# Odd block of a two-block transformer kernel: order of gate and group products, and TensorE at the borders of four stages

## The chip, the cores and the metric

The kernel runs on one core of one Trainium2 chip. The metric is the device time of one execution in microseconds; three executions of the kernel before gave 3166.43 to 3172.95, with a median of 3169.97.

## What is computed

The reference runs two small networks on one sequence of 1024 tokens with 1024 channels, all in fp32: an even and an odd mixer (`first_block`), then a gated linear attention and a forgetting attention with their gated projections (`second_block`). The change is in the odd mixer alone:

```python
def odd_mixer(h, p, on_grid):
    z = h @ p["w_in"]                                  # 1024 -> 4096
    u, g = jnp.split(z, [W_POOL], axis=-1)             # 2048 and 2048 channels
    rows = n // GRID_W
    d = multiscale_pool(u.reshape(bn * rows, GRID_W, W_POOL)).reshape(bn, n, W_POOL)
    d = d.reshape(bn, n, N_POOL_GROUPS, POOL_GROUP_DIM)    # 4 groups of 512
    y = jnp.einsum("bngi,gij->bngj", d, p["w_grp"]).reshape(bn, n, W_POOL) * p["scale"]
    return (y * jax.nn.silu(g)) @ p["w_out"]           # 2048 -> 1024
```

`multiscale_pool` takes, in group g, a mean over a window of 2, 4, 8 or 16 tokens of a row of 64, less the token itself.

## The kernel before

**Layout.** Channels lie on the 128 partitions and tokens along the free dimension, so a tensor of 1024 channels is 8 tiles of 128x1024. A product is made of fp32r parts: each operand is a high part and a low part (`h_hi`, `h_lo`), and `project` (lines 647 to 663) issues three matmuls of 128x512 for each of 8 input tiles and each half of the tokens, 48 for one output tile. A group product has only 4 input tiles (`kts=4`), so 24. Matmuls write to four PSUM slots of two banks each, `slot(0)` to `slot(3)`.

**Weight stream.** All weights pass through one stream of tiles whose order is written out in `STREAMS` (lines 35 to 50). SP loads raw tile n into `wst[n % 2]` (`load_tile`, line 485) when tile n-2 has been split (`w_split`, line 487; the DMA is line 491). GpSimd splits it into `wh` and `wl` (`split_tile`, line 566: one cast, line 585, and four quarter subtractions, line 590) when it has landed and TensorE has used tile n-2, whose buffers it takes (`w_used`, line 583). TensorE waits for the split in `take` (line 665). The order in which TensorE takes tiles is therefore also the order on SP's and on GpSimd's queue. A tile is 1024 columns wide, one for a group product is 512.

**Odd block, stages.** It runs in two parts of two groups each: `odd_a` (groups 0 and 1), `oout_a` (the output projection of their 8 y tiles), `odd_b` (groups 2 and 3), `oout_b`. In each group (`odd_groups`, line 959) TensorE makes

- u0, u1, u2, u3: four projections into slots 0 to 3. ScalarE copies each from PSUM into `up` by halves (line 1621), and VectorE pools each half in a chain of adds, one longer from group to group (lines 2322 to 2334), and splits it into `d_hi` and `d_lo` (lines 2339, 2340). A half of `up` is filled only when VectorE is done with the one before (`o_up`). VectorE signals the end of a tile's pooling with `o_d` (line 2341).
- then four times a gate projection G_j (48 matmuls, slot 2j % 4) and a group product Y_j (24 matmuls on `d`, slot (2j+1) % 4): G0 Y0 G1 Y1 G2 Y2 G3 Y3. Y0 first waits for all four pooled tiles (`o_d`, line 983). ScalarE takes the silu of G_j into `gs` (line 1629), VectorE multiplies Y_j, the scale and the silu (line 2347), signals `o_y`, splits the product into `y_hi` and `y_lo` (lines 2350, 2351) and signals `o_gs` (line 2352).

**Output projections.** `out_phase` (line 994) for `oout_a` makes 8 output tiles of 48 matmuls into slots 0 and 1 in turn. VectorE adds each to the residual stream `xr` (`residual`, line 2193, signal `x_added`), which ScalarE has loaded from DRAM at the stage's start by 8 transfers (line 1637) and stores again (line 1650). The PE waits for `x_added` of the tile two before (line 952). `oout_b` goes by halves of the tokens (`out_by_halves`, line 694): 16 steps of 24 matmuls over four banks; ScalarE loads `xr` in two transfers (line 1375), VectorE adds in line 2249, and TensorE waits for the addition of the step four before (line 701).

**Borders.** Stages are listed in `PHASES` (line 254). Each of TensorE, ScalarE and VectorE signals its end of a stage (`end`, line 263) and `begin` (line 257, its wait is line 261) lets an engine into stage k when all three have ended k-1. Before, TensorE passes such a border ahead of `oout_a`, `odd_b` and `oout_b` (lines 1003, 1005, 1007). ScalarE ends `oout_a` only when the last store of x has landed (line 1653). `xr` and `d_hi`, `d_lo` are the same memory.

Of the kernel before, what the change touches and what calls it, by code (L numbers as in the profile page):

```python
# [22 lines left out]
KT = D // P  # L23
# [8 lines left out]
KB = 1024  # L32


STREAMS = [
    ("w_even_in", 4, [1024, 1024, 1024, 512, 1024, 1024] * 2),
    ("w_even_out", 4, [1024] * 4),
    ("w_odd_in_a", 2, [1024] * 4 + [1024, 512] * 4),
    ("w_odd_out_a", 4, [1024] * 2),
    ("w_odd_in_b", 2, [1024] * 4 + [1024, 512] * 4),  # L40
    ("w_odd_out_b", 4, [1024] * 2),
    ("w_gla_rank", 1, [1024]),
    ("w_gla_in", 4, [1024] * 6),
# [64 lines left out]
def build(nc, dram, out):  # L108
# [24 lines left out]
    nm = sb("nm", 16, vend + 1024)  # L133
# [110 lines left out]
    first, n = {}, 0  # L244
# [183 lines left out]
    def _(sp):  # L428
# [80 lines left out]

        for name, times, widths in STREAMS:  # L510
            if name == "w_fox_in":
                fox_pair(0, widths)
                fox_pair(1, widths)
                with sp.Fori(0, times - 2) as i:
                    fox_pair(i + 2, widths)
                for c in range(2):
                    store_max(times - 1, c)
                    load_max(times - 1, c)
                continue
            if name == "w_even_in":  # L520

                pieces = {3: (0, 1), 4: (2, 3), 5: (4, 5), 6: (6, 7)}
                for j, w in enumerate(widths):
                    load_tile(name, 0, j, EVEN_AT[j], w, widths)
                    if j == 1:
                        for c in range(NEARLY, NCHUNK):
                            load_chunk(c)
                    if j == 3:

                        sp.wait_ge(S("h_ready"), KT)  # L530
                    for n in pieces.get(j, ()):
                        load_piece(n)
                with sp.Fori(0, times - 1) as i:
                    for j, w in enumerate(widths):
                        load_tile(name, i + 1, j, EVEN_AT[j], w, widths)
                continue
            if name == "w_even_out":
                for n, (kind, c, m) in enumerate(EVEN_OUT):
                    sp.wait_ge(S("w_split"), first[name] + n + 1)
                    b = wbuf(name, n)  # L540
                    at = (2 * kind + m % 2) * T
                    sp.dma_start(wst[b][:, :], dram[name][m // 2 * P:(m // 2 + 1) * P, at:at + T])\
                        .then_inc(S(f"w_loaded{b}"), 16)
                continue
            for half in range(passes(name)):
                with sp.Fori(0, times) as i:
                    for j, w in enumerate(widths):
                        load_tile(name, i, j, sum(widths[:j]) if name != "w_even_in" else EVEN_AT[j], w, widths,
                                  half * times * len(widths))
        sp.wait_ge(S("out_stored"), 16 * 5)  # L550

# [81 lines left out]
    def _(pe):  # L633
# [322 lines left out]
                    j += 1  # L956


        def odd_groups(part):
            nm = "w_odd_in_" + "ab"[part]  # L960

            def group(i, chase=False):
                g = 2 * part + i
                act = lambda n: pe.wait_ge(S("o_act"), 8 * g + n)
                yev = lambda n: pe.wait_ge(S("o_y"), 4 * g + n)
                if chase:
                    act(7)
                    yev(3)
                    two_tiles("eout", nm, [(0, 0), (1, 2)], lambda c: half_added("eout", 12 + c),
                              [lambda: take(nm, i, 0), lambda: take(nm, i, 1)])  # L970
                for j in range(2 if chase else 0, 4):
                    (act, yev)[j % 2](7 + j // 2 if j % 2 == 0 else 3 + j // 2)
                    take(nm, i, j)
                    project(j % 2, slot(j), h_hi, h_lo).then_inc(S("w_used"), 1)
                for j in range(4):
                    a, b = 2 * j % 4, (2 * j + 1) % 4
                    act((9, 11, 13, 14)[j])
                    take(nm, i, 4 + 2 * j)
                    project(0, slot(a), h_hi, h_lo).then_inc(S("w_used"), 1)
                    act(10) if j == 0 else act(12) if j == 1 else yev(3 + j)  # L980
                    take(nm, i, 5 + 2 * j)
                    if j == 0:
                        pe.wait_ge(S("o_d"), 4 * g + 4)
                    project(1, slot(b), d_hi, d_lo, kts=4).then_inc(S("w_used"), 1)
            if part == 0:
                group(0, chase=True)
                group(1)
            else:
                with pe.Fori(0, 2) as i:
                    group(i)  # L990
            pe.wait_ge(S("w_used"), first["w_odd_out_" + "ab"[part]] + 2)
            end(pe)

        def out_phase(nm, ready, stat, after, operand=(y_hi, y_lo)):
            with pe.Fori(0, 4) as i:
                out_pair(nm, i, [(*operand, ready)], "x_added", 2)
            pe.wait_ge(S("w_used"), first[after] + 2)
            if stat is not None:
                stats(stat)
            end(pe)  # L1000

        odd_groups(0)
        begin(pe, "oout_a")
        out_phase("w_odd_out_a", None, None, "w_odd_in_b")
        begin(pe, "odd_b")
        odd_groups(1)
        begin(pe, "oout_b")
        out_by_halves("oout_b", "w_odd_out_b", lambda c: None, (y_hi, y_lo))


        def gla_free(c):
# [307 lines left out]
    def _(act):  # L1319
# [290 lines left out]
        def odd_groups(part):  # L1610
            nm = "w_odd_in_" + "ab"[part]

            def group(i):
                g = 2 * part + i
                w0 = first[nm] + 2
                ev = lambda ins: ins.then_inc(S("o_act"), 1)
                for j in range(4):
                    act.wait_ge(S("w_used"), w0 + j + 1 + i * 12)
                    for b in range(2):
                        act.wait_ge(S("o_up"), 8 * g + 2 * j + b + 1)  # L1620
                        ins = A(up[:, :].rearrange("p (r c) -> p r c", c=80)[:, :, 8:72],  # L1621
                                bank(2 * j + b).rearrange("p (r c) -> p r c", c=64), ACT.Copy)
                        ins.then_inc(S("o_u"), 1)
                    act.wait_ge(S("o_u"), 8 * g + 2 * j + 2)
                    act.sem_inc(S("o_act"), 1)
                for j in range(4):
                    act.wait_ge(S("w_used"), w0 + 5 + 2 * j + i * 12)
                    act.wait_ge(S("o_gs"), 4 * g + j + 1)
                    ev(A(gs[j % 2][:, :], slot(2 * j % 4), ACT.Silu))
            with act.Fori(0, 2) as i:  # L1630
# [311 lines left out]
    def _(dve):  # L1942
# [366 lines left out]
        def odd_groups(part):  # L2309
            nm = "w_odd_in_" + "ab"[part]  # L2310
            v3 = lambda t: t[:, :].rearrange("p (r c) -> p r c", c=80)
            for i in range(2):
# [27 lines left out]
                        line(TT_(r3(dl), o3, r3(dh).bitcast(F32), ALU.subtract))  # L2340
                    dve.sem_inc(S("o_d"), 1)
                for j in range(4):
                    dve.wait_ge(S("w_used"), w0 + 6 + 2 * j)
                    dve.wait_ge(S("o_act"), 8 * g + 13 + j)
                    t = gs[j % 2][:, :]
                    m = 4 * i + j
# [426 lines left out]
```

## Time and profile before

| | before |
|---|---|
| median of 3 runs | 3169.97 us (3166.43 to 3172.95) |
| profiled execution, its own time | 3172.45 us |
| its span in the trace | 3170.3 us |
| mean granted TensorE clock | 0.973 of full |
| busy: TensorE, VectorE, GpSimd, ScalarE | 2962.7, 1746.6, 1316.3, 1088.0 us |
| odd block in the trace | about 847 to 1526 us |

How to read it: the profiled execution is one run, traced; its span lacks 2.2 us that its own time has around it. A row of a timeline has the start, the length, engine and line, the tiles out<-in, and in square brackets how long the engine had been idle and what ended that. Matmul records overlap: a row is 0.39 us long while the next begins 0.23 us later, and their ends are modelled.

### The profile page before, as it was taken

The numbers are of one execution on the slowest core, as the hardware profiler recorded it, in microseconds if no ns is written. First come the engines' busy times: TensorE is split into PE (matmuls) and PEld (weight loads), VectorE is DVE, ScalarE is ACT, GpSimd is POOL, SyncE is SP. The second block draws the span as 40 slices with busy tenths as digits, with TensorE's granted clock in tenths as the row PEclk, the third lists the DMA queues.
The fourth block names the chain that finished last, engine by engine and source line by source line (L and its number), as shares of the span: only waits on it lengthen the run. The fifth ranks groups of instructions, "written<-read, shape, count | busy, mean of one in ns | idle before, by whom it ended". The sixth has DMA issues, their size and how long they took to land.

```text
span 3170.3 us, 40111 instructions
## 1 busy us (share of the span) xinstructions
PE 2962.7 (93%) x13930; PEld 2287.7 (72%) x13930; DVE 1746.6 (55%) x2284; ACT 1088.0 (34%) x1429; POOL 1316.3 (42%) x1638
## 2 busy tenths in 40 slices
PE   5999999989999999989899999998999999997997
PEld 3688888757788777867688877776667666665775
DVE  7688999955545116534632322535555655556353
ACT  5344444342211000001332221324455555665232
POOL 2344454447644434436422324775221121211575
PEclk9999999999999999999899999999999999999999
DMA  7412222344311321113301103333222212221423
GB/s 298 161 63 64 63 76 73 114 151 162 102 49 44 116 80 37 47 39 137 107 27 34 33 27 106 96 87 131 54 47 54 48 33 48 48 34 41 140 82 111
DMA packets 113294, 258.56 MB, mean 82 GB/s; under 512 B 24624, under 2 KB 38000, under 8 KB 112384
## 3 DMA queue, kind: packets, MB, share of 16 engines
q1 hardware_dynamic: 83456, 189.43, 20.5%
q10 hardware_dynamic: 29696, 67.21, 5.9%
q8 instruction: 92, 1.51, 0.2%
q14 instruction: 50, 0.41, 0.0%
HBM read 223.97 MB, written 32.64 MB: 81 GB/s over the span
## 4 chain that ended last, share of the span: by engine, by line
PE 75%; DVE 11%; ACT 6%; POOL 4%; issue 3%; DMA 2%; DVEq 0%; POOLq 0%; SPq 0%; ACTq 0%
PE ps L660 20%; PE ps L661 19%; PE ps L662 19%; POOL t_wl L590 3%; PE ps L1212 2%; PE ps L1229 1%; DVE ps L2117 1%; PE ps L1027 1%; PE ps L1028 1%; PE ps L1029 1%; POOL t_wh L585 1%; DVE t_ptl L2580 1%; PE ps L1249 1%; ACT t_pr L1848 1%; DVE t_pb L2327 1%
## 5 line engine op out<-in xcount | busy, mean ns | idle before, releaser
L660 PE MATMUL ps<-t_h_hi,t_wh 128*128 128x512 f32 x2464 | 1011.6, 411 | 43.9 <-POOLq L593 13.5
L585 POOL CAST t_wh<-t_wst 128x1024 fp32r<-128x1024 f32 (+2 forms) x306 | 313.6, 1025 | 1712.1 <-PE ps L662 1538.9
L661 PE MATMUL ps<-t_h_lo,t_wh 128*128 128x512 f32 x2464 | 982.7, 399 | 0.0
L662 PE MATMUL ps<-t_h_hi,t_wl 128*128 128x512 f32 x2464 | 981.9, 398 | 0.0
L590 POOL TENSOR_TENSOR t_wl<-t_wst,t_wh 128x256 fp32r<-128x256 f32 (+2 forms) x1224 | 926.1, 787 | 24.5
L660 PEld LDWEIGHTS ps<-t_h_hi,t_wh 128*128 128x128 f32 x2464 | 467.8, 190 | 196.7 <-issue 60.5
L661 PEld LDWEIGHTS ps<-t_h_lo,t_wh 128*128 128x128 f32 x2464 | 469.0, 190 | 112.7 <-issue 8.5
L662 PEld LDWEIGHTS ps<-t_h_hi,t_wl 128*128 128x128 f32 x2464 | 467.6, 190 | 112.2
L2117 DVE SCALAR_TENSOR_TENSOR ps<-t_upad,t_vec,ps 128x1024 f32<-128x1024 f32 x224 | 275.5, 1284 | 7.1 <-DVE ps L2111 0.9
L660 PE MATMUL ps<-t_y_hi,t_wh 128*128 128x512 f32 x512 | 208.4, 407 | 21.7 <-DVEq L264 14.6
L661 PE MATMUL ps<-t_y_lo,t_wh 128*128 128x512 f32 x512 | 205.6, 402 | 0.0
L662 PE MATMUL ps<-t_y_hi,t_wl 128*128 128x512 f32 x512 | 205.2, 401 | 0.0
L1353 ACT ACTIVATE t_tmp<-t_xr 128x512 f32<-128x512 f32 x96 | 60.7, 633 | 338.6 <-DVE t_xr L2249 154.9
L1848 ACT ACTIVATE t_pr<-t_pr 128x512 f32<-128x512 f32 (+1 forms) x192 | 96.8, 522 | 225.9 <-DVE t_pr L2569 224.7
L2569 DVE SCALAR_TENSOR_TENSOR t_pr<-ps,t_negct,t_abc 128x512 f32<-128x512 f32 (+1 forms) x192 | 109.4, 611 | 68.0 <-PE ps L1233 56.2
L2580 DVE TENSOR_TENSOR t_ptl<-t_pr,t_pth 128x512 fp32r<-128x512 f32 (+1 forms) x192 | 123.1, 682 | 38.0 <-ACT t_pth L1852 37.7
L660 PEld LDWEIGHTS ps<-t_y_hi,t_wh 128*128 128x128 f32 x512 | 98.4, 192 | 50.1 <-DVEq L264 10.8
L2347 DVE SCALAR_TENSOR_TENSOR t_gs<-ps,t_vec,t_gs 128x1024 f32<-128x1024 f32 x16 | 20.5, 1284 | 188.8 <-PE ps L662 188.8
L661 PEld LDWEIGHTS ps<-t_y_lo,t_wh 128*128 128x128 f32 x512 | 98.6, 192 | 24.2 <-issue 0.7
L2554 DVE CUSTOM_DVE_ANT_0 ps<-ps,t_negc 128x512 f32<-128x512 f32 (+3 forms) x128 | 73.3, 612 | 77.5 <-PE ps L1212 44.3
L1621 ACT ACTIVATE t_up<-ps 128x512 f32<-128x512 f32 x32 | 19.2, 599 | 281.3 <-PE ps L662 150.5
L662 PEld LDWEIGHTS ps<-t_y_hi,t_wl 128*128 128x128 f32 x512 | 98.2, 192 | 24.1
(350 smaller groups left out, 4267.4 us busy)
## 6 DMA issues: line engine op xcount, KB each, us to landing
t_wst<-w_even_in SPq DMA_DIRECT2D x40, 512.0 KB, 3.5
t_wst<-w_ple SPq DMA_DIRECT2D x64, 320.0 KB, 2.9
t_wst<-w_even_out SPq DMA_DIRECT2D x32, 512.0 KB, 3.6
t_wst<-w_fox_in SPq DMA_DIRECT2D x32, 512.0 KB, 3.6
t_modw<-w_mod SPq DMA_DIRECT2D x6, 2048.0 KB, 16.2
t_xr<-x_d ACTq DMA_DIRECT2D x6, 2048.0 KB, 11.6
t_wst<-w_gla_in SPq DMA_DIRECT2D x24, 512.0 KB, 3.8
t_wst<-w_odd_in_a SPq DMA_DIRECT2D x16, 512.0 KB, 3.6
```

What stands on the lines that cost most here:

```text
L585: pool.tensor_copy(wh[b][:, 0:w], wst[b][:, 0:w]).then_inc(S("w_high"), 1)
L590: pool.tensor_tensor(wl[b][:, c], wst[b][:, c], wh[b][:, c].bitcast(F32), ALU.subtract).then_inc(S("w_low"), 1)
L660: pe.matmul(o, w1, x1, start=start and k == 0, stop=False)
L661: pe.matmul(o, w1, x2, start=False, stop=False)
L662: last = pe.matmul(o, w2, x1, start=False, stop=stop and k == kts - 1)
L1212: last = pe.matmul(bank(r + hh, 0, (hi - lo) * P), B[x][rows, a], B[y][rows, b], start=(x + y == "qhkh"), stop=(x == "ql" and hi <= t))
L1353: A(sq_half(t), xh(*divmod(t, 8)), ACT.Square).then_inc(S("half_sq"), 1)
L1848: A(pr[x][:, 0:n], pr[x][:, 0:n], ACT.Exp).then_inc(S("f_exp"), 1)
L2117: line.go(STT(out=o, in0=s, scalar=w, in1=acc[a] if o is acc[a] else by_half(acc[a]), op0=ALU.mult, op1=ALU.add))
L2554: dve.tensor_tensor_reduce(o, o, negc[hh][:, lo * P:hi * P], -1.0, 3e38 if lo == 0 else nma[hh][:, 0:1], ALU.add, ALU.min, nm[:, 8 * hh + ...
L2569: STT(out=pr[2 * (i % 2) + hh][:, 0:n], in0=bank(r + hh, 0, n), scalar=negct[:, bass.ds(16 * b + 2 * p + hh, 1)], in1=abc[hh][:, q0:q1], o ...
L2580: TT_(ptl[x][:, 0:n], pr[x][:, 0:n], pth[x][:, 0:n].bitcast(F32), ALU.subtract).then_inc(S("f_pl"), 1)
```

## The change

Two things. The stream's order in a group after the four u tiles becomes G0 G1 Y0 Y1 G2 Y2 G3 Y3 (in the columns of the weight tensor that SP reads, in TensorE's loop, and in the counts that ScalarE and VectorE wait for); the slots stay. TensorE no longer calls `begin` ahead of `oout_a`, `odd_b` and `oout_b`: ahead of the two output projections it waits until the third y product of the part's last group has left PSUM, and in the first output tile it waits ahead of each input tile for that tile of y (`y_ready`); ahead of `odd_b` it waits until the eighth residual addition is done. It still signals its ends. No arithmetic instruction is added or removed.

```diff
--- before.py
+++ after.py
@@ -32,12 +32,18 @@
 KB = 1024
 
 
+
+ODD_ORDER = [(0, 0), (0, 1), (1, 0), (1, 1), (0, 2), (1, 2), (0, 3), (1, 3)]
+ODD_AT = [1024 * j for j in range(4)] + [4096 + 1536 * j + 1024 * kind for kind, j in ODD_ORDER]
+ODD_WIDTHS = [1024] * 4 + [(1024, 512)[kind] for kind, j in ODD_ORDER]
+
+
 STREAMS = [
     ("w_even_in", 4, [1024, 1024, 1024, 512, 1024, 1024] * 2),
     ("w_even_out", 4, [1024] * 4),
-    ("w_odd_in_a", 2, [1024] * 4 + [1024, 512] * 4),
+    ("w_odd_in_a", 2, ODD_WIDTHS),
     ("w_odd_out_a", 4, [1024] * 2),
-    ("w_odd_in_b", 2, [1024] * 4 + [1024, 512] * 4),
+    ("w_odd_in_b", 2, ODD_WIDTHS),
     ("w_odd_out_b", 4, [1024] * 2),
     ("w_gla_rank", 1, [1024]),
     ("w_gla_in", 4, [1024] * 6),
@@ -545,7 +551,7 @@
             for half in range(passes(name)):
                 with sp.Fori(0, times) as i:
                     for j, w in enumerate(widths):
-                        load_tile(name, i, j, sum(widths[:j]) if name != "w_even_in" else EVEN_AT[j], w, widths,
+                        load_tile(name, i, j, ODD_AT[j] if name.startswith("w_odd_in") else sum(widths[:j]), w, widths,
                                   half * times * len(widths))
         sp.wait_ge(S("out_stored"), 16 * 5)
 
@@ -956,6 +962,10 @@
                     j += 1
 
 
+
+        def y_ready(part, k):
+            pe.wait_ge(S("o_gs"), 8 * part + 2 + k + 1)
+
         def odd_groups(part):
             nm = "w_odd_in_" + "ab"[part]
 
@@ -972,16 +982,16 @@
                     (act, yev)[j % 2](7 + j // 2 if j % 2 == 0 else 3 + j // 2)
                     take(nm, i, j)
                     project(j % 2, slot(j), h_hi, h_lo).then_inc(S("w_used"), 1)
-                for j in range(4):
-                    a, b = 2 * j % 4, (2 * j + 1) % 4
-                    act((9, 11, 13, 14)[j])
-                    take(nm, i, 4 + 2 * j)
-                    project(0, slot(a), h_hi, h_lo).then_inc(S("w_used"), 1)
-                    act(10) if j == 0 else act(12) if j == 1 else yev(3 + j)
-                    take(nm, i, 5 + 2 * j)
-                    if j == 0:
-                        pe.wait_ge(S("o_d"), 4 * g + 4)
-                    project(1, slot(b), d_hi, d_lo, kts=4).then_inc(S("w_used"), 1)
+                for n, (kind, j) in enumerate(ODD_ORDER):
+                    take(nm, i, 4 + n)
+                    if kind == 0:
+                        act((9, 11, 13, 14)[j])
+                        project(n % 2, slot(2 * j % 4), h_hi, h_lo).then_inc(S("w_used"), 1)
+                    else:
+                        act(10) if j == 0 else act(12) if j == 1 else yev(3 + j)
+                        if j == 0:
+                            pe.wait_ge(S("o_d"), 4 * g + 4)
+                        project(n % 2, slot((2 * j + 1) % 4), d_hi, d_lo, kts=4).then_inc(S("w_used"), 1)
             if part == 0:
                 group(0, chase=True)
                 group(1)
@@ -991,21 +1001,20 @@
             pe.wait_ge(S("w_used"), first["w_odd_out_" + "ab"[part]] + 2)
             end(pe)
 
-        def out_phase(nm, ready, stat, after, operand=(y_hi, y_lo)):
-            with pe.Fori(0, 4) as i:
-                out_pair(nm, i, [(*operand, ready)], "x_added", 2)
+        def out_phase(part, nm, after):
+            out_pair(nm, 0, [(y_hi, y_lo, lambda k: y_ready(part, k))], "x_added", 2)
+            with pe.Fori(0, 3) as i:
+                out_pair(nm, i + 1, [(y_hi, y_lo, None)], "x_added", 2)
             pe.wait_ge(S("w_used"), first[after] + 2)
-            if stat is not None:
-                stats(stat)
             end(pe)
 
         odd_groups(0)
-        begin(pe, "oout_a")
-        out_phase("w_odd_out_a", None, None, "w_odd_in_b")
-        begin(pe, "odd_b")
+        pe.wait_ge(S("o_y"), 4 * 1 + 7)
+        out_phase(0, "w_odd_out_a", "w_odd_in_b")
+        pe.wait_ge(S("x_added"), 2 + KT)
         odd_groups(1)
-        begin(pe, "oout_b")
-        out_by_halves("oout_b", "w_odd_out_b", lambda c: None, (y_hi, y_lo))
+        pe.wait_ge(S("o_y"), 4 * 3 + 7)
+        out_by_halves("oout_b", "w_odd_out_b", lambda c: (lambda k: y_ready(1, k)) if c == 0 else None, (y_hi, y_lo))
 
 
         def gla_free(c):
@@ -1624,7 +1633,7 @@
                     act.wait_ge(S("o_u"), 8 * g + 2 * j + 2)
                     act.sem_inc(S("o_act"), 1)
                 for j in range(4):
-                    act.wait_ge(S("w_used"), w0 + 5 + 2 * j + i * 12)
+                    act.wait_ge(S("w_used"), w0 + 5 + ODD_ORDER.index((0, j)) + i * 12)
                     act.wait_ge(S("o_gs"), 4 * g + j + 1)
                     ev(A(gs[j % 2][:, :], slot(2 * j % 4), ACT.Silu))
             with act.Fori(0, 2) as i:
@@ -2340,7 +2349,7 @@
                         line(TT_(r3(dl), o3, r3(dh).bitcast(F32), ALU.subtract))
                     dve.sem_inc(S("o_d"), 1)
                 for j in range(4):
-                    dve.wait_ge(S("w_used"), w0 + 6 + 2 * j)
+                    dve.wait_ge(S("w_used"), w0 + 5 + ODD_ORDER.index((1, j)))
                     dve.wait_ge(S("o_act"), 8 * g + 13 + j)
                     t = gs[j % 2][:, :]
                     m = 4 * i + j
```

## Rows read from the trace of the kernel before

**Rows 1.** Page, busy time: engine, us (share of span), instructions.

```profile
PE 2962.7 (93%) x13930; PEld 2287.7 (72%) x13930; DVE 1746.6 (55%) x2284; ACT 1088.0 (34%) x1429; POOL 1316.3 (42%) x1638
```

**Rows 2.** Waits of TensorE, 840 to 1620 us: us in total, times, longest.

```profile
PE ps L660 <- DVEq L2341: 21.7, 2, 13.9
...
PE ps L660 <- DVEq L264: 9.2, 2, 4.7
```

**Rows 3.** Timeline of TensorE: six restarts, and three starts ahead of them.

```profile
869.31 0.48 PE L660 MATMUL ps<-t_h_hi,t_wh 128*128 128x512 f32 x1 [1.81 <-POOLq L593]
...
1072.50 0.39 PE L662 MATMUL ps<-t_d_hi,t_wl 128*128 128x512 f32 x1
...
1077.61 0.49 PE L660 MATMUL ps<-t_y_hi,t_wh 128*128 128x512 f32 x1 [4.72 <-DVEq L264]
...
1173.84 0.79 PE L660 MATMUL ps<-t_h_hi,t_wh 128*128 128x512 f32 x1 [4.83 <-ACTq L264]
...
1239.31 0.77 PE L660 MATMUL ps<-t_d_hi,t_wh 128*128 128x512 f32 x1 [7.71 <-DVEq L2341]
...
1353.94 0.40 PE L662 MATMUL ps<-t_h_hi,t_wl 128*128 128x512 f32 x1
...
1368.28 0.76 PE L660 MATMUL ps<-t_d_hi,t_wh 128*128 128x512 f32 x1 [13.94 <-DVEq L2341]
...
1425.69 0.39 PE L662 MATMUL ps<-t_d_hi,t_wl 128*128 128x512 f32 x1
...
1430.52 0.79 PE L660 MATMUL ps<-t_y_hi,t_wh 128*128 128x512 f32 x1 [4.44 <-DVEq L264]
```

**Rows 4.** Windows: stretch, its us, TensorE busy us (matmuls), granted clock, DMA share, GB/s.

```profile
910.13:921.33 11.20, 11.20 (x49) 1.00 0.20 68
...
869.31:882.13 12.82, 12.82 (x48) 0.87 0.22 63
...
1077.61:1090.45 12.84, 12.84 (x48) 0.87 0.93 346
...
1173.84:1186.64 12.80, 12.80 (x48) 0.87 0.15 42
...
1239.31:1247.77 8.46, 8.46 (x24) 0.64 0.19 59
...
1368.28:1375.52 7.24, 7.24 (x24) 0.76 0.00 0
...
1430.52:1444.56 14.04, 14.04 (x48) 0.78 0.94 334
```

**Rows 5.** Timeline of VectorE, pooling of group 3: starts of four halves, last instruction.

```profile
1341.00 0.82 DVE L2322 TENSOR_TENSOR t_pa<-t_up 128x632 f32<-128x632 f32 x1 [0.15 <-DVE t_d_lo L2340]
...
1347.73 0.82 DVE L2322 TENSOR_TENSOR t_pa<-t_up 128x632 f32<-128x632 f32 x1
...
1353.83 0.82 DVE L2322 TENSOR_TENSOR t_pa<-t_up 128x632 f32<-128x632 f32 x1 [0.15 <-DVE t_d_lo L2340]
...
1362.13 0.82 DVE L2322 TENSOR_TENSOR t_pa<-t_up 128x632 f32<-128x632 f32 x1
...
1367.38 0.69 DVE L2340 TENSOR_TENSOR t_d_lo<-t_pa,t_d_hi 128x512 fp32r<-128x512 f32 x1
```

**Rows 6.** Timeline of GpSimd: split of the tile taken when Y3 is used.

```profile
1427.37 4.21 POOL L590 TENSOR_TENSOR t_wl<-t_wst,t_wh 128x256 fp32r<-128x256 f32 x4
```

**Rows 7.** Timeline of VectorE: first and last residual of oout_a, first of oout_b.

```profile
1092.83 1.28 DVE L2193 SCALAR_TENSOR_TENSOR t_xr<-ps,t_modv,t_xr 128x1024 f32 x1 [15.72 <-DMA t_xr<-x_d]
...
1169.29 1.28 DVE L2193 SCALAR_TENSOR_TENSOR t_xr<-ps,t_modv,t_xr 128x1024 f32 x1 [9.92 <-PE ps L662]
...
1440.73 0.75 DVE L2249 SCALAR_TENSOR_TENSOR t_xr<-ps,t_modv,t_xr 128x512 f32<-128x512 f32 x1 [9.13 <-DMA t_xr<-x_d]
```

**Rows 8.** Timeline of SP: issue of raw tile 3 of oout_b.

```profile
1431.79 0.33 SPq L491 DMA_DIRECT2D t_wst<-w_odd_out_b  x1
```

**Rows 9.** DMA issues: the same transfer, its KB and us to landing.

```profile
t_wst<-w_odd_out_b SPq DMA_DIRECT2D x1, 512.0 KB, 7.7
```

## Prediction

> **What bounds the kernel now.** The page first: TensorE is busy for 2962.7 of 3170.3 us [rows 1], so what counts is when it waits and at which clock it starts again. Next the waits of TensorE in the odd block: two waits for the pooled tiles (signal `o_d`, line 2341) hold 21.7 us, two for VectorE's end of a stage (line 264) hold 9.2 us [rows 2]; the timeline adds a third border, where ScalarE ends last, 4.83 us [rows 3]. Last, the windows behind each restart: a full tile of 48 matmuls takes 11.20 us at granted clock 1.00 (2.4 GHz), but 12.80 to 14.04 us behind a wait, where the granted clock falls to the lower level, 1.2 GHz, for a while (0.78 to 0.87 on average over the window) [rows 4]. The odd block loses time to five waits and to five slow restarts; the rest of it is a closed row of matmuls.
>
> A wait is counted here as the idle time in brackets plus 0.16 us, because a record is 0.39 us long where the next matmul follows after 0.23 us. The five are, in this order: `oout_a` 4.88, `odd_b` 4.99, Y0 of group 2 7.87, Y0 of group 3 14.10, `oout_b` 4.60 us [rows 3]. The slow restarts cost 1.64, 1.60, 2.86 (8.46 less 5.60), 1.64 (7.24 less 5.60) and 2.84 us [rows 4].
>
> **Part 1, G1 ahead of Y0.** It puts 11.20 us of matmuls [rows 4] into the wait for `o_d`.
>
> Group 2 waits 7.87 us, less than 11.20: the wait goes, 3.33 us are to spare, and with it goes the slow restart. Gain 7.87 + 2.86 = 10.73 us. Groups 0 and 1 have no such wait that is worth a row; gain 0.
>
> Group 3 waits 14.10 us. G0 begins its last matmul at 1353.94 and Y0 starts at 1368.28 [rows 3]; VectorE ends its pooling at 1368.07 [rows 5]. So 14.10 - 11.20 = 2.90 us stay. The pooling also gets later, since GpSimd's split slows VectorE: a half takes 6.10 us (1347.73 to 1353.83) with no split beside it, 6.73 (1341.00 to 1347.73) beside that of a tile of 512, 8.30 (1353.83 to 1362.13) beside one of 1024 [rows 5]. In the new order G1's split (1024) stands where Y0's (512) was and the other way round, which cancels; but G1 is used 11.2 us after G0, at about 1365.4, and Y1's split (512) falls on the end of the last half. By the row that is 0.63 us. What stays is about 3.5 us; gain 10.6 us. The slow restart behind it stays too, since waits of 4.4 to 13.9 us all had one; I keep its 1.64 us, and 2.86 is the other end, 1.2 us worse.
>
> The price is on the weight stream. Y0 and Y1 stand together, so G2's split can begin only when Y0 is used and must be done in Y1's 5.60 us, while VectorE works on y0. The nearest row is the split behind Y3 of the last group, with VectorE at y7: last matmul of Y3 at 1425.69 [rows 3], split done at 1427.37 + 4.21 = 1431.58 [rows 6], 5.89 us later; SP sees it 0.21 us later [rows 8]. G2 would be due 5.83 us after that start, so it is 0.3 us late, in each of 4 groups: -1.2 us. Ends: 0 and -2.4. Y1's split (512) has Y0's 5.60 us and an idle VectorE for cover in three groups; cost 0. Gone cover would cost what a split of 512 lasts beyond it. SP loads on the split of the tile two before, so the loads of the moved tiles stay a tile ahead; the issue at 1431.79 is 0.21 us behind such a split [rows 6, 8]. The waits of ScalarE and VectorE only take new counts: silu 1 may begin before y0, as `gs` has two buffers; nothing else is queued behind it. Cost 0.
>
> **Part 2, the borders.** `oout_a`: slot 0 and slot 1 are free when Y3 ends, its weights are split, and seven y tiles are there. They give 7 x 6 matmuls, 9.8 us, and y7 is ready at the latest when the old restart came, 4.88 us in. So the wait and its restart go, 4.88 + 1.64. TensorE still waits for its own last matmul (`w_used` ahead of `end`, line 991), which no row shows alone: 0.16 us of drain and some 0.2 to 0.4 us of signal and weight load; I take 0.5, ends 0.2 and 1.0. What is late next: tile 2 needs the residual of tile 0, which needs all of x. x is loaded at the same moment as before, when VectorE ends, and is there at 1092.83; with 1.28 us of addition [rows 7] and 0.2 of signal that is 1094.3. Tile 2 would now be due at 1072.73 + 0.5 + 22.4 = 1095.6, a margin of 1.3 us. But one more raw tile, 512 KB, now comes while x (4096 KB, for which VectorE waited 15.72 us [rows 7]) still loads: at the same rate 2.0 us. I take 0.3 us of stall, ends 0 and 2. Gain 5.7 us.
>
> `odd_b`: TensorE now waits for the eighth residual alone: 1169.29 + 1.28 [rows 7] + 0.2 = 1170.8 in place of 1173.84 [rows 3]. Gain 3.07 us. Some 1.76 us of idle stay. Does the clock fall for so little? The nearest restart, 1.81 us of idle at 869.31 [rows 3], was slow, 12.82 us for 48 matmuls [rows 4]; so nothing is gained, and 1.60 is the other end. ScalarE and VectorE enter later than TensorE, but their first work is 11 us off. That cover is whole.
>
> `oout_b`: the first step has 7 x 3 matmuls before y7, 4.9 us, and y7 comes 4.60 us in: no wait, but a thin margin (0.3 plus the 0.5 of drain). Gain 4.60 + 2.84 - 0.5 = 6.94 us. Late next: raw tile 3 is issued at 1431.79 and takes 7.7 us, beside the load of x [rows 8, 9], so it lands at 1439.5. Step 3 is now due at 1425.92 + 0.5 + 3 x 5.6 = 1443.2. A split has 4.21 us of subtractions beside a busy VectorE [rows 6] and a cast of about 1.1 us ahead of them (1427.37 less Y3's end at 1425.92 and the signal): ready at 1444.8 + 0.2 at the latest, and with VectorE idle until 1440.7 about 1.1 us sooner, 1443.9. -0.7 us, ends 0 and -1.8. The first residual is possible at 1440.73 [rows 7], and its sum is first needed by step 4 at 1449; cost 0.
>
> **The sum.** 10.73 + 10.6 - 1.2 + 5.7 + 3.07 + 6.94 - 0.7 = 35.1 us. From the profiled execution's own 3172.45 us that leaves 3137.3; the median of the runs is 2.48 us below that execution, so on its basis 3134.9, rounded to **3135 us**. Behind the odd block everything follows TensorE, so nothing is given back there. A difference of under 0.2% (6.3 us) could not be told from none.
>
> **Rivals.**
>
> A. x is the bound. TensorE comes to the output projections up to 4.9 us earlier, x does not. For it: margin of 1.3 us in `oout_a`, DMA share 0.93 and 0.94 in both stages [rows 4]. Against: it needs x 5 us later than now. If both borders' gains (5.7 and 6.2) come back as stalls with slow restarts: 3135 + 12 = 3147. Chance 0.07.
>
> B. GpSimd and VectorE exclude each other. If one of the splits' five instructions held VectorE up for its whole length, Y1's split would cost group 3 not 0.63 us but its GpSimd time, and as the pooling has some 3 us left by then, about 3 us: 3138. Against it: a half beside a whole split of 1024 is only 2.2 us longer [rows 5]. Chance 0.07. The Trainium skill, "SBUF — State Buffer", section "SBUF: two separate sides", speaks for it: the port pair that GpSimd and VectorE share is a lock, and the one that comes second is blocked until the first one's instruction ends. By that rule the sum would be the 3138 above, by the rows 3135.
>
> C. The new waits are no earlier than the old. If the wait on its own products or on y kept TensorE out until VectorE ends its stage, only part 1 would gain, 20.1 us: 3150. For it: TensorE still counts its own tiles ahead of `end`. Against: none of these signals is VectorE's last. Chance 0.03.
>
> D. Slower. The weight stream becomes the bound of the pair Y0, Y1, if the raw tiles of Y1 and G2 are issued only when the tile ahead of their buffer is used, not when it is split. Then a landing (up to 7.7 us [rows 9]) and a split (up to 5.9 us) lie in 5.6 us of cover, twice: 2 x 8.0 us in each group, 64.0 in all, against the 36.3 gained before the price of the splits: 3170 + 28 = 3198. It decides against the change from 9.1 us a group on. Against: issues follow the split by 0.21 us [rows 6, 8]. Chance 0.02.
>
> E. Less clock is lost than taken: 1.76 us of idle leave the clock up at `odd_b`, the splits are in time: 3135 - 1.6 - 1.2 - 1.0 = 3131. Chance 0.09.
>
> **How the numbers follow.** The forecast has 0.70, 3131 to 3140 by itself; with A to E that is 0.98, and 0.02 is for what I do not see. All but D and part of the last are faster by far more than 0.2%: faster 0.96, same 0.02, slower 0.02. The range: all upper ends together (restart 1.2, stall at x 1.7, raw tile 1.1, splits 1.2, pooling 2.4, drain 1) are 8.6, the lower ones about 5, and runs scatter by 3 us either way: 3128 to 3145. That takes in B and E and leaves out A, C and D.
>
> **What would show it.** In the profile of the changed kernel: no wait for line 2341 in group 2, and one of 3 to 4.5 us in group 3 (none: the pooling got faster; over 6: B); four waits of 0.1 to 0.5 us for GpSimd ahead of G2; gaps under 1 us at `oout_a` and `oout_b`, 1.5 to 2 us at `odd_b`, there with a mean clock of about 0.87 in the first tile; no wait of TensorE for x or for an addition in tile 2 of `oout_a` over 1 us. Wrong is the forecast if TensorE still stands for 4 us at a border, or if the wait in group 2 is only moved to Y1 or G2.

## Result and the profile after

The changed kernel takes 3130.66 us (median of 4 runs, 3128.44 to 3134.87) against 3171.46 us for the kernel before (4 runs, 3166.43 to 3173.81): ratio 0.9875, 95% interval 0.9858 to 0.9892. Two later jobs timed it again, with ratios of 0.9885 (0.9862 to 0.9907) and 0.9898 (0.9883 to 0.9913). The profiled execution took 3134.87 us, 37.6 less than that of before. Forecast were 3135 us and 35.1 us less; between the medians lie 40.8 us in this job, 36.3 and 33.9 in the two later ones.

Waits of TensorE in the changed kernel, 830 to 1590 us (us in total, times, longest), against [rows 2]. Lines have moved: 2341 is now 2350, 593 is 599, 264 is 270.

```profile
PE ps L666 <- POOLq L599: 3.4, 3, 1.8
PE ps L666 <- DVEq L2350: 3.3, 1, 3.3
...
PE ps L666 <- DVE t_xr L2202: 1.9, 1, 1.9
...
PE ps L666 <- PE ps L668: 0.7, 2, 0.4
```

The 21.7 us of waits for the pooled tiles are now 3.3, once; the three waits for a border are gone, and 1.9 (the last residual) and 0.7 (TensorE's own last product) stand in their place. The same in the timeline of TensorE, against [rows 3]; the last three rows, out of the order of time, are the last matmul of Y1 and the first of G2 in group 2, and step 3 of `oout_b`:

```profile
870.71 0.48 PE L666 MATMUL ps<-t_h_hi,t_wh 128*128 128x512 f32 x1 [1.81 <-POOLq L599]
...
1073.62 0.47 PE L666 MATMUL ps<-t_y_hi,t_wh 128*128 128x512 f32 x1 [0.41 <-PE ps L668]
...
1165.35 0.49 PE L666 MATMUL ps<-t_h_hi,t_wh 128*128 128x512 f32 x1 [1.90 <-DVE t_xr L2202]
...
1348.52 0.73 PE L666 MATMUL ps<-t_d_hi,t_wh 128*128 128x512 f32 x1 [3.31 <-DVEq L2350]
...
1395.83 0.47 PE L666 MATMUL ps<-t_y_hi,t_wh 128*128 128x512 f32 x1 [0.30 <-PE ps L668]
...
1243.62 0.40 PE L668 MATMUL ps<-t_d_hi,t_wl 128*128 128x512 f32 x1
1244.14 0.49 PE L666 MATMUL ps<-t_h_hi,t_wh 128*128 128x512 f32 x1
...
1413.65 0.50 PE L666 MATMUL ps<-t_y_hi,t_wh 128*128 128x512 f32 x1 [0.79 <-POOLq L599]
```

G2 starts 0.52 us after the matmul ahead of it, where 0.23 is the pace: 0.29 us late. A slow restart is a stretch of matmuls at the lower clock behind a wait. The windows behind four restarts, against [rows 4] (stretch, its us, TensorE busy us (matmuls), granted clock, DMA share, GB/s). The kernel before has a granted clock of 0.87, 0.87 and 0.78 where the first, second and last have 1.00:

```profile
870.71:881.91 11.20, 11.20 (x48) 1.00 0.33 95
1165.35:1176.55 11.20, 11.20 (x48) 1.00 0.27 94
1348.52:1361.66 13.14, 13.00 (x48) 0.87 0.07 20
1395.83:1407.03 11.20, 11.20 (x48) 1.00 0.63 215
```

Only the restart behind the 3.31 us was slow, by 13.14 - 11.20 - 0.30 (the late G2 at its end) = 1.64 us.

**A measure that scatters less.** The time of a whole run moves by 3 to 6 us either way. The odd block has two marks in the trace, the last statistics matmul of the even output projection and the first of `oout_b`. In the kernel before:

```profile
845.90 1.02 PE L686 MATMUL ps<-t_rs,t_vec 128*128 128x512 f32 x2
...
1481.81 1.13 PE L686 MATMUL ps<-t_rs,t_vec 128*128 128x512 f32 x2 [0.69 <-DVEq L2254]
```

and in the changed one:

```profile
847.30 1.02 PE L692 MATMUL ps<-t_rs,t_vec 128*128 128x512 f32 x2
...
1445.40 1.12 PE L692 MATMUL ps<-t_rs,t_vec 128*128 128x512 f32 x2 [0.68 <-DVEq L2263]
```

This odd stretch was 635.9 us and is 598.1: 37.8 less. What lies outside it in the span, 2534.4 before and 2534.6 after, holds nothing of the change, and it scatters: 2532.8 and 2528.7 in the two later profiles of the changed kernel, 2528.5 to 2537.3 in all. The table has all profiles; slow restarts are counted where matmuls of 128x512 follow each other by 0.43 us, not 0.23.

| kernel | odd stretch, us | slow restart behind the 1.8 us of idle at group 0 | behind the 1.9 at `odd_b` |
|---|---|---|---|
| before | 635.9 | yes | (4.8 of idle) yes |
| changed | 598.1 | no | no |
| changed, again | 599.7 | no | yes |
| changed, third | 597.7 | no | no |
| order only | 615.5 | yes | (4.8 of idle) yes |
| borders only | 619.3 | yes | no |
| u0 early | 596.4 | no | (0.5 of idle) no |
| G2 too ahead | 596.7 | yes | yes |
| x late | 608.5 | yes | yes |
| second half of x later | 600.5 | yes | yes |
| no wait for own product | 597.1 | no | no |
| four edits | 592.8 | yes | (0.5 of idle) no |
| late raw tiles | 642.8 | (6.4 of idle) yes | no |

### The profile page after: what moved, and what is told of

The parts are those of the page before. It is cut to its first block, busy times and chain, and to the rows that moved or that the text cites. A ratio compares the mean times of both kernels' runs of the same rounds, so it can differ in the third digit from the quotient of the medians.

```text
span 3132.7 us, 40108 instructions
## 1 busy us (share of the span) xinstructions
PE 2955.4 (94%) x13930; PEld 2280.3 (73%) x13930; DVE 1750.7 (56%) x2284; ACT 1088.1 (35%) x1429; POOL 1314.6 (42%) x1638
## 4 chain that ended last, share of the span: by engine, by line
PE 74%; DVE 9%; ACT 6%; POOL 4%; issue 3%; DMA 2%; DVEq 0%; POOLq 0%; SPq 0%; ACTq 0%
PE ps L666 20%; PE ps L668 19%; PE ps L667 19%; POOL t_wl L596 3%; PE ps L1221 2%; PE ps L1238 1%; POOL t_wh L591 1%; DVE ps L2126 1%; PE ps L1036 1%; PE ps L1037 1%; PE ps L1038 1%; DVE t_pr L2578 1%; ACT t_pr L1857 1%; DVE t_ptl L2589 1%; PE ps L1106 1%
## 5 line engine op out<-in xcount | busy, mean ns | idle before, releaser
L666 PE MATMUL ps<-t_h_hi,t_wh 128*128 128x512 f32 x2464 | 1010.8, 410 | 38.4 <-DVE t_h_lo L2230 6.9
L667 PEld LDWEIGHTS ps<-t_y_lo,t_wh 128*128 128x128 f32 x512 | 97.0, 189 | 23.5 <-issue 0.7
## 6 DMA issues: line engine op xcount, KB each, us to landing
t_modw<-w_mod SPq DMA_DIRECT2D x6, 2048.0 KB, 16.2
```

What stands on the lines that cost most here:

```text
L666: pe.matmul(o, w1, x1, start=start and k == 0, stop=False)
L667: pe.matmul(o, w1, x2, start=False, stop=False)
```

## Experiments

**The new order alone** (`e1_order_only`):

```diff
         odd_groups(0)
-        pe.wait_ge(S("o_y"), 4 * 1 + 7)
+        begin(pe, "oout_a")
         out_phase(0, "w_odd_out_a", "w_odd_in_b")
-        pe.wait_ge(S("x_added"), 2 + KT)
+        begin(pe, "odd_b")
         odd_groups(1)
-        pe.wait_ge(S("o_y"), 4 * 3 + 7)
+        begin(pe, "oout_b")
```

> The new order of gates and group products, with the three stage borders of TensorE as before. Theory (the gain is the sum of the waits and slow restarts): group 2 gives 10.7 us, group 3 10.6 us, less 1.2 us for four late splits: 20.1 us faster than before, about 3151. TensorE waits about 3.5 us for the pooled tiles in group 3 and not in group 2; the three border waits of 4.4 to 4.9 us stand. Rival (part of the 40.8 us measured between the medians comes from the clock in other stages, not from the change): the waits are the same but the time is off the sum by several us either way, and the trace shows other slow restarts outside the odd block.

Measured: 3146.59 us, ratio 0.9931 (0.9915 to 0.9948), and an odd stretch 20.4 us shorter than before. Some of its waits of TensorE:

```profile
PE ps L666 <- DVEq L270: 8.9, 2, 4.4
PE ps L666 <- ACTq L270: 4.8, 1, 4.8
PE ps L666 <- DVEq L2350: 3.3, 1, 3.3
```

The borders are as before, and of the pooling one wait of 3.3 us is left. The stretch is within 0.3 us of the 20.1 of the sum; its slow restart at `odd_b` was 1.3 us longer than before and the one at `oout_b` 1.2 shorter, which cancels. The median gave 23.5 us in that job, more than the sum, within the runs' scatter (3145.9 to 3153.8). The rival is right in this much: outside the stretch this profile spent 5.9 us less than that of before, which no wait of the odd block explains. Two profiles of the unedited changed kernel differ there by as much, so that part of a difference of medians is scatter.

**The new borders alone** (`e2_borders_only`):

```diff
-ODD_ORDER = [(0, 0), (0, 1), (1, 0), (1, 1), (0, 2), (1, 2), (0, 3), (1, 3)]
+ODD_ORDER = [(0, 0), (1, 0), (0, 1), (1, 1), (0, 2), (1, 2), (0, 3), (1, 3)]
```

> The old order of gates and group products, with the new waits at the three borders. Theory: 5.9 us at oout_a, 2.9 at odd_b, 6.0 at oout_b = 14.9 us faster, 16.5 if the clock stays up behind the 1.9 us of idle at odd_b; about 3156. The waits for the pooled tiles stay at 7.9 and 14.1 us. Rival (the two parts do not add, because TensorE's earlier start at odd_b only lengthens its wait for VectorE's pooling in group 2): the wait in group 2 grows to about 10.8 us and the gain is some 3 us less, about 3159.

Measured: 3155.69 us, ratio 0.9950 (0.9933 to 0.9966), 14.4 us below the median of before, and a stretch 16.6 us shorter than before. Some of its waits:

```profile
PE ps L666 <- DVEq L2350: 21.6, 2, 13.9
...
PE ps L666 <- DVE t_xr L2202: 1.9, 1, 1.9
```

The waits for the pooled tiles are 21.6 us, 21.7 before: they did not grow when TensorE came to `odd_b` earlier, as it must be if VectorE's pooling follows u0 and not the border. The rival of this run falls. There was no slow restart at `odd_b`: 14.9 + 1.6 = 16.5 was the expected gain for that case. Of the 16.6, 0.6 is luck: the restart in group 2 was 1.4 us shorter than before, the one in group 3 0.8 longer. The two parts give 20.4 + 16.6 = 37.0 us, the whole change 37.8: they add, to within the price of one slow restart.

**u0 of `odd_b` after the seventh residual** (`e3_u0_early`):

```diff
-        pe.wait_ge(S("x_added"), 2 + KT)
+        pe.wait_ge(S("x_added"), 1 + KT)
         odd_groups(1)
...
                 for j in range(2 if chase else 0, 4):
+                    if part == 1 and j == 1:
+                        pe.wait_ge(S("x_added"), 2 + KT)
```

> The changed kernel, but TensorE begins u0 of odd_b after the seventh residual addition (its slot 0 is free then) and waits for the eighth only ahead of u1. Theory (the idle of 1.9 us at odd_b is a pure wait for PSUM that u0 does not need): the 1.9 us go, 3128.7 against the changed kernel's 3130.7, and no slow restart can occur there. Rival (ScalarE and VectorE enter odd_b later than TensorE and the time comes back as a wait for them): no change, with a new wait ahead of u1 or Y0.

Measured: the idle at the border is 0.49 us and not none, no wait comes later in its place, and the odd stretch is 596.4 us, 1.7 less than in the changed kernel's first profile, 1.4 of it at the border. The median, 3133.97 us where 3128.7 was expected, shows nothing of it: the changed kernel itself gave 3130.7, 3133.1 and 3137.1 in three jobs.

**G2 too ahead of Y0** (`e4_g2_ahead`):

```diff
-ODD_ORDER = [(0, 0), (0, 1), (1, 0), (1, 1), (0, 2), (1, 2), (0, 3), (1, 3)]
+ODD_ORDER = [(0, 0), (0, 1), (0, 2), (1, 0), (1, 1), (0, 3), (1, 2), (1, 3)]
```

> The changed kernel with G2 too ahead of Y0: G0 G1 G2 Y0 Y1 G3 Y2 Y3. Theory: 11.2 us more cover the 3.5 us that group 3 still waits for pooling, so that wait and its slow restart (1.65) go; a second late split of about 0.25 us per group (the next tile after Y2, behind Y3) costs 1.0: about 4.1 us faster than the changed kernel, 3126.6. Rival (the weight stream is near its limit and a second pair of short products tips it): TensorE waits for GpSimd by over 1 us per group, and the kernel is no faster than 3130.

Its waits of TensorE, 880 to 1440 us:

```profile
PE ps L666 <- DVE t_xr L2202: 1.9, 1, 1.9
PE ps L666 <- POOLq L599: 1.6, 4, 0.7
```

The pooling is covered in all four groups, and GpSimd's four waits sum to 1.6 us, one of them the known 0.7 at step 3 of `oout_b`. The stretch is 596.7 us with two slow restarts that the changed kernel's first profile did not have; at 1.6 us each it is 4.6 us shorter, where 4.1 was expected. The rival's waits of over 1 us per group did not come. The median, 3131.13, was expected at 3126.6 by the theory and not under 3130 by the rival; taken alone it would speak for the rival, but medians of one kernel differ by more than these two figures do.

**The changed kernel again** (`after_again`, no edit):

> The changed kernel once more, unedited, to see what scatters. Read in the trace: the odd stretch, from the last statistics matmul of the even output projection to the first one of oout_b (635.9 us before, 598.1 in the changed kernel's first profile). Theory: the waits are the same to 0.1 us, and only which of the waits are followed by a slow stretch of matmuls varies; behind the two idles of 1.8 and 1.9 us it may or may not come, behind the one of 3.3 us it comes. The stretch is 598 to 601. Rival (the clock follows from the schedule alone): every slow restart stands where it stood and the stretch is 598.1 to 0.2 us.

Measured: 3133.13 us, ratio 0.9885. Its waits in the odd stretch are those of the first profile to 0.05 us, but the stretch is 599.7 us. The same idle of 1.90 us at `odd_b` has this behind it:

```profile
1163.27:1176.07 12.80, 12.80 (x48) 0.87 0.24 82
```

12.80 us at a mean granted clock of 0.87, where the first profile has 11.20 at 1.00. So whether the clock falls to 1.2 GHz behind such an idle does not follow from the schedule alone; the rival falls.

**Raw tiles issued on use** (`e6_late_loads`):

```diff
             sp.wait_ge(S("w_split"), first[name] + before + j + i * len(widths) + 1)
+            if name.startswith("w_odd_in"):
+                sp.wait_ge(S("w_used"), first[name] + before + j + i * len(widths) + 1)
```

> The changed kernel, with SP issuing a raw tile of the odd input streams only when the tile two before has been used, not when it has been split. It measures the rival in which the stream bounds the pair Y0, Y1. A landing (3.6 us) and a split then follow each use: about 1.1 us late at Y1, 2.6 at G2 and at G3, 2.6 at u0 of groups 1 and 3, so 25 + 5 = 30 us, and up to 1.6 more at each wait that is followed by a slow stretch: 3161 to 3175. The rival's own price (landing 7.7, split 5.9, twice a group) would give 64 us, 3195.

Measured: 3177.87 us (one run), a stretch of 642.8 us, 44.7 more than in the changed kernel. Some of its waits, 880 to 1440 us:

```profile
PE ps L668 <- POOLq L601: 27.6, 11, 3.1
PE ps L668 <- DVEq L2352: 3.3, 1, 3.3
```

Ten waits of 2.1 to 3.1 us give 29 us, and six of them had a slow restart, 10.5 us together. Group 0's u2 waits 6.4 us in place of 1.8, with a slow restart of 2.7 us, which had not been counted; the four late G2 and the wait at step 3 are gone in exchange, some 2.5 us. The run is therefore 3 us above the range that was expected. One of these waits is 2.7 us on average, as expected, and not the 8.0 of rival D, which took a landing of 7.7 us where 3.6 is usual. The slower side exists, above the kernel before, and it hangs on one thing: that SP is let go by the split and not by the use.

**x loaded later in `oout_a`** (`e7_x_late`):

```diff
             begin(act, name)
+            act.wait_ge(S("w_used"), first["w_odd_out_a"] + 2 + 1)
             out_load(x_d)
```

> The changed kernel, with ScalarE starting the load of x in oout_a when TensorE has used the first output tile, some 7 us later than now. It takes away the margin that the new start left (x landed 0.7 us ahead of need in the changed kernel's trace). Theory: x lands about 7 us later, TensorE waits at output tile 2 for the first residual, 6.3 us and perhaps a slow restart of 1.6 to 2.8, and all of it stays: 3137 to 3140. Rival (the stage has slack and takes it up): no more than 1 us.

In the changed kernel VectorE's first residual waits for x:

```profile
1093.86 1.28 DVE L2202 SCALAR_TENSOR_TENSOR t_xr<-ps,t_modv,t_xr 128x1024 f32 x1 [16.38 <-DMA t_xr<-x_d]
```

x has landed when VectorE starts at 1093.86, and output tile 2 is due at 1073.62 + 22.40 = 1096.02; the residual of 1.28 us leaves it 0.7 to spare after 0.2 of signal (by the same reckoning 1.2 and 1.6 in the two later profiles). In this one TensorE's timeline has:

```profile
1103.88 0.79 PE L666 MATMUL ps<-t_y_hi,t_wh 128*128 128x512 f32 x1 [5.83 <-DVE t_xr L2203]
```

and VectorE's the residual that it waited for:

```profile
1102.46 1.28 DVE L2203 SCALAR_TENSOR_TENSOR t_xr<-ps,t_modv,t_xr 128x1024 f32 x1 [23.19 <-DMA t_xr<-x_d]
```

A wait of 6.0 us and a slow restart; the run took 3142.93 us and the stretch 608.5 us, 10.4 more than the changed kernel's. Of that, 6.0 and 1.5 are this wait, and the two other slow restarts hold the rest; with them the run lies 3 us above the 3137 to 3140 that was expected. The stage has no slack: rival A's mechanism is real, and the change passes it by 0.7 to 1.6 us.

**The second half of x later in `oout_b`** (`e8_x_second_half_later`):

```diff
-        def load_x(src):
+        def load_x(src, halves=(0, 1)):
...
-        load_x(x_d)
+        load_x(x_d, (0,))
         for t in range(16):
             squares_of("oout_b", t)
+            if t == 0:
+                load_x(x_d, (1,))
```

> The changed kernel, with ScalarE loading the second half of x for oout_b after the first square, not along with the first half. Theory (raw tile 3 lands late because it shares the DMA engines with 4 MB of x): it lands in under 6 us, the wait of 0.8 us at step 3 goes, and the first residual comes some 5 us sooner; 0.8 us less in the odd stretch. Rival (the tile is late because it is issued late): the wait stays at 0.8 us.

Measured: raw tile 3 took 7.4 us to land, 7.9 in the changed kernel, and the wait at step 3 is 0.32 us, 0.79 there. The halves of x (2 MB each) land in this run 9.4 us after their issue, one after the other; in the changed kernel, where they are issued 0.45 us apart, the first lands after 9.9 us and the second after 16.2. The first row is of this run, the second of the changed kernel, with the median of its two:

```profile
t_xr<-x_d ACTq DMA_DIRECT2D x2, 2048.0 KB, 9.4
...
t_xr<-x_d ACTq DMA_DIRECT2D x2, 2048.0 KB, 13.1
```

So the expectation was wrong: the second half takes only some 0.5 us from the first and from raw tile 3, and the first residual comes 0.5 us sooner after the load's issue and not 5. It is the tile behind, raw tile 4, that gains: 4.6 us to land, 6.9 in the changed kernel. In the third profile of the unedited kernel the wait at step 3 was 0.41 us, so even the 0.5 us that it lost here are within what it varies by. Raw tile 3 is beside the first half of x in either kernel, and no run took that half away; that it sets the tile's landing is not shown.

**No wait for the own last product** (`e10_no_own_wait`):

```diff
-            pe.wait_ge(S("w_used"), first["w_odd_out_" + "ab"[part]] + 2)
             end(pe)
```

> The changed kernel without TensorE's wait for its own last product ahead of its end of odd_a and odd_b. Theory (that wait drains the array and exposes a signal and a weight load): the gaps of 0.81 and 0.70 us at oout_a and oout_b fall to about 0.25, together 1.0 us. Rival (the gap is the first wait for y or the weights' split, not this one): they stay above 0.6.

The first output matmul follows at the pace of the stream:

```profile
1070.21 0.39 PE L668 MATMUL ps<-t_d_hi,t_wl 128*128 128x512 f32 x1
1070.44 0.40 PE L666 MATMUL ps<-t_y_hi,t_wh 128*128 128x512 f32 x1
```

Both gaps, 0.81 and 0.70 us, are gone, so the rival falls; the stretch is 597.1 us, 1.0 less as expected, and the run took 3128.68 us.

**Four edits together** (`e9_all`: `e3_u0_early`, `e4_g2_ahead`, `e8_x_second_half_later` and `e10_no_own_wait`), with the changed kernel beside it on the same chip (`after_third`):

> Four small edits on the changed kernel together: u0 of odd_b after the seventh residual, G2 too ahead of Y0, the second half of x for oout_b later, and no wait of TensorE for its own last product ahead of its end of odd_a and odd_b. Theory: 1.4 us (idle at odd_b down from 1.9 to 0.5), 3.5 + 1.65 less 1.0 (group 3), 0.5 (raw tile 3) and up to 0.7 (own products) add to 5 to 7 us in the odd stretch, besides 1.6 wherever a slow restart is absent that the changed kernel sometimes has: a stretch of about 592, and a median 5 us below that of the changed kernel in this job. Rival (what is taken from one wait comes back at the next tile of the weight stream): no more than 2 us.

> The changed kernel once more beside the version with the four edits, on the same chip, for a comparison of medians: 3130 to 3134, some 5 us above that version by the theory, within 2 us of it by the rival. In its trace: waits as in the two profiles before to 0.1 us, an odd stretch of 598 to 601, depending on slow restarts behind the idles of 1.8 and 1.9 us.

Measured: 3124.86 us (3122.59 to 3129.51, 5 runs), ratio 0.9853 (0.9840 to 0.9867) to the kernel before, against 3137.13 us (3128.62 to 3141.20, 4 runs), ratio 0.9898 (0.9883 to 0.9913), for the changed kernel, whose median had been expected at 3130 to 3134. Waits of TensorE in the four edits, 840 to 1442 us:

```profile
PE ps L666 <- POOLq L599: 2.2, 3, 1.8
...
PE ps L666 <- PE ps L668: 0.5, 1, 0.5
```

and in the changed kernel's third profile:

```profile
PE ps L666 <- DVEq L2350: 3.3, 1, 3.3
PE ps L666 <- POOLq L599: 2.2, 2, 1.8
PE ps L666 <- DVE t_xr L2202: 1.9, 1, 1.9
...
PE ps L666 <- PE ps L668: 0.7, 2, 0.4
```

The stretch is 592.8 us, with the slow restart of group 0 in it, and 597.7 in the other without: 4.9 us shorter, 6.5 with that restart set aside. The rival, which had at most 2 us, falls with the stretch. Of the 12 us between the medians, where 5 were expected, the traces explain about half. That the other half is scatter outside the odd block is not shown: the two profiled executions differ by 5.9 us there, but the other way. The intervals of this job do not overlap, but that of the changed kernel's first job (0.9858 to 0.9892) overlaps with that of the four edits. It is the lowest median here.

## Why the prediction was right

All terms of the sum have their counterpart, in the kernel before and the changed kernel's first profile:

| term | predicted, us | measured, us | from |
|---|---|---|---|
| group 2, wait and restart | 10.73 | 10.73 | both gone |
| group 3, wait | 10.6 | 10.62 | 14.10 to 3.48 |
| `oout_a`, wait and restart | 5.7 | 5.94 | 6.52, less a gap of 0.81 over the pace of 0.23 |
| `odd_b`, wait | 3.07 | 2.93 | starts 5.22 apart, now 2.29 |
| `odd_b`, restart | 0 | 1.60 | 12.80 to 11.20 |
| `oout_b` | 6.24 | 6.02 | 7.44, less 0.47 and the 0.95 at step 3 |
| late G2, four groups | -1.2 | -1.05 | 0.23, 0.23, 0.29, 0.30 |
| restart behind group 0 | none | 1.62 | slow before, not after |

The measured terms sum to 38.4 us where the stretch is 37.8 shorter. The 0.6 left stands behind the seven new short gaps (four late G2, two own products, step 3): the second matmul after each comes 0.30 to 0.34 us after the first, not 0.23.

**Step by step.** The wait that stays in group 3 was put at 3.5 us, 2.90 from the cover and 0.6 from GpSimd's split beside the last half: 3.31 us of idle and 0.16 for the record make 3.47, the same within 0.01 us in seven of the nine profiles with that order (the idle was 3.13 and 3.25 us in the other two). The start of VectorE's last half but three and its last half in the changed kernel, then GpSimd's split beside the last half, and one with VectorE idle:

```profile
1320.70 0.82 DVE L2331 TENSOR_TENSOR t_pa<-t_up 128x632 f32<-128x632 f32 x1 [0.15 <-DVE t_d_lo L2349]
...
1341.93 0.82 DVE L2331 TENSOR_TENSOR t_pa<-t_up 128x632 f32<-128x632 f32 x1
...
1345.16 0.69 DVE L2341 TENSOR_TENSOR t_pb<-t_pb,t_vec 128x512 f32<-128x512 f32 x1
1345.89 0.98 DVE L2343 TENSOR_TENSOR t_pa<-t_pb,t_up 128x512 f32<-128x512 f32 x1
...
1347.50 0.82 DVE L2349 TENSOR_TENSOR t_d_lo<-t_pa,t_d_hi 128x512 fp32r<-128x512 f32 x1
...
1346.40 2.65 POOL L596 TENSOR_TENSOR t_wl<-t_wst,t_wh 128x128 fp32r<-128x128 f32 x4
...
916.62 1.71 POOL L596 TENSOR_TENSOR t_wl<-t_wst,t_wh 128x128 fp32r<-128x128 f32 x4
```

The last half took 1348.32 - 1341.93 = 6.39 us, against 5.94 before (1362.13 to 1368.07 [rows 5]), with no split beside it. So the split, of which some 2.9 us fell beside this half, cost it 0.45 us, not 3, and rival B did not come. The three halves ahead of it took 21.23 us, 21.13 before, so the two splits that changed places did cancel, but for 0.1 us; with it the measured 3.47 is 2.90 + 0.45 + 0.1. The 0.6 came out partly by luck, with a term of 0.63 that was 0.45.

The Trainium skill, "SBUF — State Buffer", section "SBUF: two separate sides", has the second of the two engines blocked until the first one's instruction ends. These rows don't refute that: VectorE's 0.98 and 0.82 us stand where 0.69 is usual, and GpSimd's four subtractions took 2.65 us, 1.71 with VectorE idle, so each engine held the other up, instruction by instruction. What the 0.45 us refutes is rival B's price, for which VectorE would have had to stand for the whole split.

Part 2's cover held (y7, the split of the first weights and the first residual were all in time), by the margin of 0.7 us that `e7_x_late` took away. The 2.0 us that one more raw tile beside x was to cost were too many: VectorE's wait for x was 15.72 us before [rows 7] and 16.38, 15.93 and 15.47 in the three profiles of the changed kernel, and the 0.3 us of stall in the sum did not come. The late G2 came from where it was said, the split in Y1's 5.60 us; in group 3 it ends at 1357.21 + 4.27 = 1361.48, and G2 starts at 1361.66:

```profile
1357.21 4.27 POOL L596 TENSOR_TENSOR t_wl<-t_wst,t_wh 128x256 fp32r<-128x256 f32 x4
```

Rival C fell with the timeline, rival D with `e6_late_loads`, which shows that its mechanism is there once the loads are let go by the use.

**What was off** is the restart behind the short idle at `odd_b`. The text took the nearest row, 1.81 us of idle with a slow restart, for the rule, with 1.60 us as the other end. The same idle at the same place was slow in 7 of 12 profiles, and the new one of 1.90 in 4 of 9; it is a toss, and the first profile had it the good way twice. The two are 3.2 us, more than the 2.7 that lie between 35.1 and 37.8. One sign that the prediction named, a mean clock of about 0.87 in the first tile of `odd_b`, was therefore absent in the first profile and there in the second. The 3130.66 us of the first job, 4 below the forecast, are not a term that was missed: the three jobs gave 3130.7, 3133.1 and 3137.1 for one kernel, around the 3135 that was forecast. 3131 is also the number of rival E, but of E's two conditions only the clock at `odd_b` held, in the first profile; the splits were late, by 1.05 us for G2 and 0.95 at step 3. E's third term, 1.0 us, has no source in its text. That the forecast fits this closely is in part luck, since the medians scatter by more than its error.

## What to carry to other kernels

Where the engine that bounds the kernel waits for a chain of another, move work of its own into the wait and count the cover in its own durations: here 11.2 us went into 7.9 and 14.1, and what was left came out within 0.1 us. A border that all engines cross together is worth its wait and the slow matmuls behind it, but an engine that crosses early takes margin from every transfer that still starts at the border; look which is next (here 0.7 to 1.6 us). For edits of a few microseconds compare the stretch between two marks in the trace, since three medians of one kernel lay 6.5 us apart.

## What the runs showed of the hardware

Behind an idle of TensorE of 1.8 to 1.9 us the granted clock fell in 11 of 21 cases and stayed in 10; behind those of 2.1 to 3.1 us in `e6_late_loads` it fell in six of ten; behind every idle of over 3.1 us in the odd stretch it fell. The price of a fall was 5 to 8 matmuls of 128x512 at 0.43 us instead of 0.23, 1.4 to 1.7 us, or 11 to 13 of them, 2.5 to 2.9 us, with no relation to the length of the idle: in the kernel before 2.9 us behind 7.7 and 1.6 behind 13.9, in `e2_borders_only` 1.5 behind 7.7 and 2.5 behind 13.9.

Raw tile 3 of `oout_b`, 512 KB, took 6.8 to 8.0 us in all profiles beside a load of x, where 3.6 is the median of the stream. With one transfer of 2 MB in flight it was 7.4 and 6.9 us, with two 6.8 to 8.0. Of two transfers of 2 MB issued 0.45 us apart the first landed after 9.9 us, little later than alone (9.4), and the second after 16.2.

VectorE and GpSimd slow each other while both run: four subtractions of 128x128 on GpSimd took 2.65 us and not 1.71, VectorE's 128x512 up to 0.98 and not 0.69.
